# Reordered seam between sample sequences, head norms by logarithm and exponential, token rows by GpSimd's queue and VectorE

## The reference, cut to what matters

```python
def rms_norm(x, g):
    xf = x.astype(F32)
    y = xf * lax.rsqrt(jnp.mean(xf * xf, axis=-1, keepdims=True) + EPS)
    return (y * g.astype(F32)).astype(x.dtype)

k = rms_norm(k.reshape(bsz, L, N_HEADS, 2, HEAD_DK), k_norm)        # head norms of k, q, o
q = rms_norm((h @ w_q).reshape(bsz, L, N_HEADS, 2, HEAD_DK), q_norm)
...
# prompt: causal, 4 blocks of 128 queries; sample: 2048 cached keys and 8 new ones
p = jax.nn.softmax(s, axis=-1)
w = p[:, :, 0] - lam * p[:, :, 1]
o = w @ v
...
o = rms_norm(o, subln) * (1.0 - lam_init)
```

## Time and profile before

| | |
|---|---|
| median of 3 runs | 2074.89 us (2073.44 to 2076.32) |
| the profiled execution, own time | 2083.15 us |
| its span | 2081.3 us |
| PE, PEld, DVE, ACT, POOL busy | 89%, 80%, 40%, 35%, 7% |
| mean granted PE clock | 0.927 |
| `dense("q")`; `qtok` and GpSimd's set-up; attention; `ohead` | 976 to 1024.7; 1024.7 to 1074; 1074 to 1530; 1530 to 1565 us |

### The profile page before, as it was taken

How to read it: one execution, slowest core, us unless ns; L and a number is a source line. 1 busy time by engine, 2 the same in 40 slices (tenths; PEclk the granted TensorE clock), 3 DMA queues, 4 the chain that set the end, 5 groups by cost and what they waited for, 6 DMA issues and landing times.

```text
span 2081.3 us, 42740 instructions
## 1 busy us (share of the span) xinstructions
PE 1851.6 (89%) x17223; PEld 1659.0 (80%) x17223; DVE 839.7 (40%) x1423; ACT 734.0 (35%) x1112; POOL 142.5 (7%) x277
## 2 busy tenths in 40 slices
PE   4798889899999999898868888988758799999998
PEld 2473679799999999798856766666438799999997
DVE  6557223433333233315764444444454433333232
ACT  1433333433333222424346444444131333333212
POOL 2010012200000022101010000000013200000000
PEclk9878899899999999899989999999868799999999
DMA  8758642122222223222158888888651122222222
GB/s 241 261 186 285 210 134 81 51 78 84 81 81 76 70 83 96 61 81 61 61 170 278 324 317 310 306 305 303 217 162 51 51 81 81 81 81 70 82 83 73
DMA packets 245005, 301.03 MB, mean 145 GB/s; under 512 B 10188, under 2 KB 195472, under 8 KB 244816
## 3 DMA queue, kind: packets, MB, share of 16 engines
q1 hardware_dynamic: 241752, 290.22, 42.5%
q10 hardware_dynamic: 2432, 8.16, 1.1%
q0 software_dynamic: 704, 0.95, 0.2%
HBM read 291.92 MB, written 7.37 MB: 144 GB/s over the span
## 4 chain that ended last, share of the span: by engine, by line
PE 71%; DVE 10%; DMA 7%; ACT 4%; SPq 4%; issue 3%; POOL 0%; DVEq 0%; ACTq 0%; POOLq 0%
PE ps L576 55%; PE ps L499 5%; DMA kpg<-in_cache_k 3%; DVE t L1761 2%; SPq L449 2%; DMA raw<-in_w_ada_mix 2%; PE ps L526 2%; SPq L456 2%; PE ps L860 2%; PE ps L715 1%; DMA vpg<-in_cache_v 1%; PE ps L931 1%; DMA raw<-in_w_ada_ffn 1%; ACT kTs L1341 1%; DVE wh L1701 1%
## 5 line engine op out<-in xcount | busy, mean ns | idle before, releaser
L576 PE MATMUL ps<-hr,ws 128*128 128x288 f32 x5760 | 787.2, 299 | 34.8 <-DVE hr L1719 16.9
L576 PEld LDWEIGHTS ps<-hr,ws 128*128 128x128 f32 x5760 | 782.6, 192 | 38.7 <-issue 31.4
L1713 DVE TENSOR_TENSOR ws<-raw,ws 128x1024 fp32r<-128x1024 f32 x200 | 234.8, 1176 | 699.9 <-ACT ws L1189 699.9
L1189 ACT ACTIVATE ws<-raw 128x1024 fp32r<-128x1024 f32 x200 | 201.2, 1008 | 656.9 <-PE ps L576 632.0
L576 PE MATMUL ps<-gr,ws 128*128 128x288 f32 x2112 | 279.4, 294 | 0.0
L576 PEld LDWEIGHTS ps<-gr,ws 128*128 128x128 f32 x2112 | 279.1, 188 | 0.0
L1341 ACT ACTIVATE kTs<-ps 128x512 f32<-128x512 f32 x256 | 141.2, 596 | 165.5 <-PE ps L499 165.1
L499 PE MATMUL ps<-ident,kpg 128*128 128x128 f32 x1024 | 152.7, 298 | 15.7 <-DMA kpg<-in_cache_k 10.6
L499 PEld LDWEIGHTS ps<-ident,kpg 128*128 128x128 f32 x1024 | 123.1, 152 | 46.6 <-issue 23.1
L526 PE MATMUL ps<-raw,cond 128*32 128x256 f32 x896 | 83.5, 482 | 44.7 <-DMA raw<-in_w_ada_mix 34.6
L576 PE MATMUL ps<-hg,ws 128*128 128x288 f32 x768 | 106.2, 302 | 8.9 <-DVE ws L1713 8.9
(11 more groups left out here) (312 smaller groups left out, 1595.2 us busy)
## 6 DMA issues: line engine op xcount, KB each, us to landing
kpg<-in_cache_k SPq DMA_DIRECT2D x128, 512.0 KB, 5.7
vpg<-in_cache_v SPq DMA_DIRECT2D x128, 512.0 KB, 5.9
raw<-in_ffn_w SPq DMA_DIRECT2D x88, 512.0 KB, 3.8
raw<-in_w_ada_mix SPq DMA_DIRECT2D x48, 512.0 KB, 5.4
raw<-in_w_ada_ffn SPq DMA_DIRECT2D x48, 512.0 KB, 4.8
raw<-in_ffn_w SPq DMA_DIRECT2D x48, 384.0 KB, 3.5
raw<-in_w_ada_kv SPq DMA_DIRECT2D x16, 512.0 KB, 5.6
raw<-in_ssm_w_glu SPq DMA_DIRECT2D x16, 512.0 KB, 4.3
```

The lines of the kernel that those rows point to most:

```text
L576: return mm(ps[:, 4 * s + 2 * tile + h, 0:HALF], ws[:, (u * S + j) % 2, w, k, :], src[:, k0 + k, v, h * HALF:(h + 1) * HALF], start=(k0 + ...
L1189: A(ws[:, w, 0, 0:nk, :].rearrange("p k n -> p (k n)"), raw[:, slot, 0:nk, :].rearrange("p k n -> p (k n)"), ACT.Copy).then_inc(slab_high, 1)
L1713: TT(f(ws[:, w, 1, 0:nk, :]), f(raw[:, slot, 0:nk, :]), f(ws[:, w, 0, 0:nk, :]).bitcast(F32), ALU.subtract).then_inc(raw_done[slot], 1)
```

## The change

1. **Head norms.** `head_root` becomes `Ln` (out of PSUM into `t2`), a semaphore wait on `ln_head`, and `Exp` with scale -0.5 in place: exp(-0.5 ln(m + eps)). DVE's `RECIPROCAL` goes, and with it one step.
2. **qtok.** The five V copies go from ACT to DVE, each behind the head norm of the same unit. All ten stores go from ACT's queue to GpSimd's, which issues them in a loop ahead of its set-up for attention. `y` gets its own semaphores.
3. **The seam on PE.** `block_weights` of a head's last block goes to the end of the turn, behind `new_scores(b)`. `outputs(b)` goes behind `turn_page(b+1, 0)` and `turn_weights(b+1, 0)`, which change places. `values(b, 0)` now waits for `o_ready`.
4. **The seam on DVE.** `outputs` is split: `values_out(b)` (L1919) ahead of `bias(b)`, the rest behind `weights(b+1, 0)`. `block_turned` of a head's last block goes to the end of the turn. `normalize` goes from the start of the turn to behind `block_weights` of its first block.

```diff
@@ PE, sequence
+                if keys:
+                    turn_page(b, par, 0)
                 if vals:
                     turn_weights(b, par, 0)
-                if keys:
-                    turn_page(b, par, 0)
+                if b > LAG:
+                    outputs(b - 1)
                 for u in range(PAGES):
...
-                    if u % 4 == 0 and 0 < n <= H * QB:
+                    if u % 4 == 0 and u and 0 < n <= H * QB:
                         block_weights(n - 1)
...
                 if keys:
                     new_scores(b, par)
-                if vals:
-                    outputs(b)
+                if 0 < n0 + QB <= H * QB:
+                    block_weights(n0 + QB - 1)
@@ ACT
             def head_root(n, bank, s, width):
                 act.wait_ge(head_ready, n + 1)
-                return A(halves(t2[:, s, :]), ps[:, bank:bank + 2, 0:HALF], ACT.Sqrt, bias=eps[:, 0:1], scale=1.0 / width)
+                A(halves(t2[:, s, :]), ps[:, bank:bank + 2, 0:HALF], ACT.Ln, bias=eps[:, 0:1], scale=1.0 / width).then_inc(ln_head, 1)
+                act.wait_ge(ln_head, n + 1)
+                return A(t2[:, s, :], t2[:, s, :], ACT.Exp, scale=-0.5)
@@ GpSimd, ahead of its set-up for attention
+            for n in range(2 * (QB + 1)):
+                s, v, i = n % 2, n // (QB + 1), n % (QB + 1)
+                pool.wait_ge(free[s], uses("qtok", s, n // 2) + 1)
...
+                pool.dma_start(rows_.rearrange(form), dst).then_inc(tok_put[i % 2], 16)
@@ DVE
             def head(src, h, s, g):
-                step(REC(t2[:, s, :], t2[:, s, :]))
...
+            for n in range(2 * (QB + 1)):
+                s, v, i = n % 2, n // (QB + 1), n % (QB + 1)
+                if n < H:
+                    dve.wait_ge(root_head, n + 1)
+                    head(qT, n, s, vec[:, 121:122])
+                if v:
+                    wait_unit(dve, "qtok", s, n // 2)
...
+                    if i == QB:
+                        dve.wait_ge(tok_put[i % 2], 16 * 5)
+                    CP(dst, ps[0:NTOK[i], 4 * s + 2:4 * s + 4, :].rearrange("p b c -> p (b c)")).then_inc(free[s], 1)
@@ DVE, sequence
                     weights(b, 0)
-                if 0 < b <= DB:
-                    normalize(b, par)
+                if b > LAG:
+                    outputs(b - 1)
...
-                    if 0 < n <= H * QB:
+                    if q and 0 < n <= H * QB:
                         block_turned(n - 1)
...
                         block_weights(n)
+                    if q == 0 and 0 < b <= DB:
+                        normalize(b, par)
                     if keys:
                         scores(b, par, q)
                 if keys:
                     new_scores(b, par)
+                if vals:
+                    values_out(b)
+                if keys:
                     bias(b)
-                if vals:
-                    outputs(b)
+                if 0 < n + 1 <= H * QB:
+                    block_turned(n)
```

More of the change, by code:

```diff
@@ L924, in values @@
                 if u == 0:
-                    pe.wait_ge(o_copied, b - LAG + 1)
+                    pe.wait_ge(o_ready, b - LAG + 1)
                 if u % 4 == 0:
@@ L981, in sequence @@
                     new_scores(b, par)
-                if vals:
-                    outputs(b)
+                if 0 < n0 + QB <= H * QB:
+                    block_weights(n0 + QB - 1)
             for b in range(DB + LAG):
                 sequence(b)
+            outputs(DB + LAG - 1)
             pe.wait_ge(o_ready, DB + 1)
@@ L1302, in _ @@
                     head_root(H + n, 4 * s, s, DK).then_inc(root_head, 1)
[L1303 to L1309, removed]
+                if not v:
+                    if i >= 2:
+                        act.wait_ge(tok_put[slot], 16 * (i // 2))
+                    A(tok[0:NTOK[i], slot, :], ps[0:NTOK[i], 4 * s + 2:4 * s + 4, :].rearrange("p b c -> p (b c)"), ACT.Copy
+                      ).then_inc(free[s], 1)
                 if n + 2 < H:
                     square(qT, n + 2, s)
[L1312 to L1317, removed]
             def block_exp(n):
@@ L1514, in _ @@
             apply("q")
+            for n in range(2 * (QB + 1)):
+                s, v, i = n % 2, n // (QB + 1), n % (QB + 1)
+                pool.wait_ge(free[s], uses("qtok", s, n // 2) + 1)
+                o_ = out[6 + v] if i < QB else out[8 + v]
+                rows_ = (o_[0, i * P:(i + 1) * P] if i < QB else o_)
+                form = {(0, 0): "t h m d -> t (h m d)", (0, 1): "t h d -> t (h d)", (1, 0): "b t h m d -> (b t) (h m d)",
+                        (1, 1): "b t h d -> (b t) (h d)"}[(int(i == QB), v)]
+                dst = vtok[:, i].rearrange("p h d -> p (h d)") if v and i < QB else tok[0:NTOK[i], i % 2, :]
+                pool.dma_start(rows_.rearrange(form), dst).then_inc(tok_put[i % 2], 16)
             pool.wait_ge(head_ready, 2 + 2 * H)
@@ L1767, in dense @@
                 S, n0 = len(slabs), SLABS[name] - DENSE0
-                steps_ = per * {"glu": 1, "q": 1}.get(name, 0)
+                steps_ = per * {"glu": 1}.get(name, 0)
                 def turn(i, last):
@@ L1829, in _ @@
             dense("q", tail=False)
-            for n in range(H):
-                dve.wait_ge(root_head, n + 1)
-                head(qT, n, n % 2, vec[:, 121:122])
+            for n in range(2 * (QB + 1)):
[5 more added lines that the diff above has]
+                    wait_unit(dve, "qtok", s, n // 2)
+                    dst = vtok[:, i].rearrange("p h d -> p (h d)") if i < QB else tok[0:NTOK[i], i % 2, :]
+                    if i == QB:
+                        dve.wait_ge(tok_put[i % 2], 16 * 5)
+                    CP(dst, ps[0:NTOK[i], 4 * s + 2:4 * s + 4, :].rearrange("p b c -> p (b c)")).then_inc(free[s], 1)
             def block_max(n):
@@ L1914, in weights, with values_out, outputs @@
                 CP(wT[:, q % 2, :], ps[:, 7, :]).then_inc(wt_copied, 1)
-            def outputs(b):
+            def values_out(b):
                 dve.wait_ge(vn_used, b - LAG + 1)
                 CP(osb[:, :], ps[:, 6, 0:2 * DV]).then_inc(o_copied, 1)
+            def outputs(b):
                 dve.wait_ge(o_turned, b - LAG + 1)
@@ L1943, in sequence @@
                     new_scores(b, par)
+                if vals:
+                    values_out(b)
+                if keys:
                     bias(b)
-                if vals:
-                    outputs(b)
+                if 0 < n + 1 <= H * QB:
+                    block_turned(n)
             for b in range(DB + LAG):
                 sequence(b)
+            outputs(DB + LAG - 1)
             split(SLABS["wo"] - DENSE0)
             split(SLABS["wo"] - DENSE0 + 1)
-            with step.loop(0, H // 2, 2) as i:
+            with dve.Fori(0, H // 2) as i:
                 for s in range(2):
```

11 lines of the change are left out of this document (6 added, 5 removed).

## The result

The changed kernel takes 2049.61 us (median of 4 runs, 2047.03 to 2051.1) against 2074.97 before: ratio 0.9877, 95% interval 0.986 to 0.9894. That is 25 us or 1.2% faster; the forecast was 2052. The profiled execution of the changed kernel took 2049.9 us, at its median, while that of before lay 8 us above its own. So I compare stages, not spans. Times of stages are of one profiled execution each.

The account below looks back on a forecast made before the run. PE was taken to bound the attention, with holes at the seams, and DVE's head-norm chains `qtok` and `ohead`. Seams -44.4 and norms with token rows +21.3 gave -23.1, from 2074.9 to 2051.8 us; range 2018 to 2080.

Parts of the forecast that it names:

- Two loads a head: Head norms: `Ln` and `Exp` taken to sit in different tables, so two loads a head, 1.28 us each.
- The slower rival: Table switches hold ScalarE longer than the load's row: 2106 us; chance 0.15, shared with a sum off that far.
- The first pair of the q product, +4.6: In `dense("q")`, loads around the first pair's norms free set 0 at 983.8 in place of 979.2.
- qtok: Norms and token rows: last `Exp` 39.0 us after first `Ln`, first scores +13.5 us, including +4.3 from the first pair.
- ohead: Head norms of the output: ACT at 4.62 or 5.19 us a head, ending 7.8 us later.
- The seams, -48.4: Attention, between turns: the new order removes PE's holes and half clock, gaining 48.4 us over eight seams.
- the walk: PE and DVE followed through seam 4 to 5 at full clock: 7.9 us in place of 15.8; other seams likewise.
- `normalize`, +4.0: Late `normalize` on DVE delays PE's second `block_scores`: 0.4 x 6 = 2.4 us, plus 1.6 in turn 8.
- The rest of the attention: Attention outside the seven seams; the whole attention was forecast at 48.4 - 4.0 = 44.4 us gained.
- The transfers take over: Rival: page loads hold the turn near 51 us, the seams give half, 22: 2074 us; chance 0.13.
- The sum: Whole kernel: -44.4 from the seams and +21.3 from norms and token rows, -23.1 us in all.
- its own range: Likeliest case's range, 2037 to 2073 us: from half clock staying in part and 9.6 of `normalize`, to no stall there.

Follow-up runs that it names:

- e4: The changed kernel with one line more, loading the table with both logarithm and exponential ahead of the q product: 2004.4 us.
- e5: The changed kernel with `normalize` back at the start of the turn, ahead of the first `block_max`: 2044.1 us.
- e0: The kernel before, unchanged, run again for a second profile: 2076.2 us.
- e2: The kernel before with only the head norms changed to logarithm and exponential, token rows left on ScalarE: 2094.3 us.
- e3: The kernel before with only the token rows moved, V copies to DVE and stores to GpSimd's queue: 2083.7 us.
- e1: The kernel before with only the seam's reordering on PE and DVE (parts 3 and 4): 2030.3 us.
- e8: The changed kernel with both the one table loaded ahead and `normalize` at the start of the turn: 2004.4 us.
- e6: The kernel before with only the seam's part for `wtT`, `outputs(b)` staying directly behind `new_scores(b)`: 2046.7 us.
- e9: The changed kernel with one table loaded ahead, `normalize` early, and V copies and their stores back on ScalarE: 1996.4 us.

## Why the prediction was right, step by step

- **Two loads a head.** Right, 48 of them, each 1.283 us with work starting 0.02 behind it. The choice rested on loads being placed without looking ahead; e4 shows that a table with both functions exists and that, with the load placed by hand ahead of the loop, none is placed inside it. The slower rival (a switch costs more than its row) is out: `Ln` starts 1.30 us after its load does (1044.69 to 1045.99), as in rows 10. The Trainium skill (ScalarE: Activation LUTs, section "Table sets: the hidden batching unit") has one load for `ln` then `exp`; the trace of the changed kernel differs, with 48 loads for 24 pairs, and e4, where the set with both is named, agrees with it, with no load in its 24 pairs. The Trainium skill (ScalarE: Activation LUTs, section "What ACT_TABLE_LOAD costs") adds a drain of about 1.38 us to each load; the trace differs, with 1.30 us from the start of a load of 1.28 to the start of `Ln`, and 0.02 from the end of `Ln` to the next load.
- **The first pair of the q product, +4.6.** Measured 4.8, by other parts. The reload at the loop head cost nothing: it ran at 972.0, while ACT waited for PE. The first products resumed 3.2 us later in the stage, and 1.6 more came from the clock: the same 45 products ran at 1.00 before and at a mean of 0.78 behind the longer hole. The changed kernel, then the kernel before:

```profile
972.00 1.28 ACT L1193 ACT_TABLE_LOAD   x1
...
979.50 7.77 PE L577 MATMUL ps<-hr,ws 128*128 128x288 f32 x45 [3.96 <-ACT t L1237]
```

```profile
979.20 6.20 PE L576 MATMUL ps<-hr,ws 128*128 128x288 f32 x45 [0.75 <-DVE ws L1713]
```

- **qtok.** First `Ln` to last `Exp` 39.0 forecast, 39.2 measured (1034.93 to 1074.11); from there to the scores 10.6 and 10.75; in all +13.5 and +13.9.
- **ohead.** +7.8 and +7.8.
- **The seams, -48.4.** Right in mechanism, and near in sum: the seven seams that the walk prices at -47.8 took 99.9 us before and 52.3 after, -47.6. Single seams were off both ways:

| seam (turns) | before, us | after, us | gain forecast | gain measured |
|---|---|---|---|---|
| 1 to 2 | 11.8 | 8.7 | 4.3 | 3.0 |
| 2 to 3 | 13.8 | 6.65 | 6.0 | 7.2 |
| 3 to 4 | 17.0 | 6.65 | 9.1 | 10.3 |
| 4 to 5 | 15.8 | 6.65 | 7.9 | 9.1 |
| 5 to 6 | 15.7 | 6.65 | 7.8 | 9.1 |
| 6 to 7 | 15.7 | 8.2 | 7.8 | 7.5 |
| 7 to 8 | 10.2 | 8.8 | 4.9 | 1.4 |

  Four seams are 1.2 to 1.3 us shorter than forecast, since PE has no gaps between its groups: it is busy 6.60 of 6.60 us, with PEld's 5.34 under it. The forecast had gaps of 1.5 us. (The walk as written does not add up either: from 1299.1 its terms and 1.5 of gaps end at 1306.9, and its 1306.0 leaves 0.6 for them.) The three others are dearer than forecast because the clock was not at full: its mean was 0.80, 0.79 and 0.61, and the last seam's `head_values` took 4.64 us, not 2.4. The first and the last of them also have about 1 us of waits each. The seam from 6 to 7 has no hole at all. Its eight page transposes:

```profile
1376.80 1.91 PE L500 MATMUL ps<-ident,kpg 128*128 128x128 f32 x8
```

  Here are the sums over the seven seams, before and after. The waits in them fell from 32.2 to 2.2 us, and PE's busy time by 17.6:

```profile
sum 99.92, PE 67.69 PEld 50.31 DVE 34.05 ACT 28.13 POOL 2.62; mean PE 9.67 PEld 7.19 DVE 4.86 ACT 4.02 POOL 0.38
```

```profile
sum 52.29, PE 50.12 PEld 39.83 DVE 21.89 ACT 27.25 POOL 2.62; mean PE 7.16 PEld 5.69 DVE 3.13 ACT 3.89 POOL 0.37
```

- **`normalize`, +4.0.** Right in mechanism (DVE's queue, covered in part by page loads). The waits of `block_scores` for `wtT` came to 9.1 us in the attention, after 1.2 before: 0.87 in each of the turns 2 to 7 where I had 0.4, and 3.0 in turn 1, which I had left out. But waits for pages shrank beside them. Outside these seams PE's waits grew by 1.8 us in all (32.6 to 34.4), and undoing the step in e5 saved 1.6 of waits. So the net cost is below the 4.0, not above.
- **The rest of the attention.** Measured -51.2 against -44.4. The missing 6.8 us lie outside the seven seams, where I expected 3.4 us more and the trace has 3.5 less: PE's busy time there fell from 323.7 to 318.5 us for the same products. That need not come from the change. The same stretches kept PE busy for 324.0, 318.1 and 317.7 us in e0, e2 and e3, which have the kernel before's order, and for 320.5 and 320.3 in e1 and e4, which have the changed one. It is the clock, which differs between executions of one order.
- **The transfers take over.** Not in this kernel, but near. The share over a turn is 0.99, and SP issues 29 pages from 1293.83 to 1330.82, one in 1.32 us: for 32 pages 42 of the 45.8 us. (In rows 7 the last load shown is the 29th too, not the thirtieth, so the pace there was 1.31, not 1.26; and the share in rows 8 is 1.02, where the prediction read 1.00.) The waits of e5 and e8 show that most of what the early `normalize` saves inside a turn is lost to the loads.
- **The sum.** Forecast -23.1. By the stages -51.2 + 13.9 + 7.8 = -29.4; by the medians -25.4; e1 and e2 alone, by medians, -45.8 + 18.2 = -27.6. Against e0, whose own time is near the median, the stages give -28.6 and the parts ahead and behind 2.3 back. That the forecast lies within 2.3 us of the median is in part luck: seams off both ways cancelled, and so did, in part, the clock outside the seams and the wandering of parts that no edit touches. The lower end of its own range, 2037, has no sum behind it: no stall at `normalize` leads only to 2048.

## What to carry to other kernels

Cost an activation together with its table: where two functions alternate, count two loads per pair unless a table with both is active, and look at the program for the loads; one load placed by hand was worth 45 us here, more than the whole change. Look at the granted clock when you price a short hole on TensorE: in e6 a hole of 1.8 us cost 4.0 on average, since the clock fell behind it, and in the seams of this change 30.1 us of waits were worth 47.6. Before you look for the cause of a few us, compare PE's busy time and clock for the same products: here they differed by 7 us (e8 and e9) with the waits the same. When an instruction of another engine seems to set the length of a wait, follow what is ahead of it in its own queue: it may move up with the engine that waits.

## What the runs showed of the hardware that I had not expected

- A hole of 1.8 us on TensorE, with small products of 8 columns ahead of it, is followed by half clock for a stretch: in all five seams of e6 from turn 2 to turn 7 (mean clock 0.70 or 0.83). Of the same five seams of the changed kernel, which have no hole, four ran at 1.00. The fifth fell to half clock all the same, behind the same small products (mean 0.79, 8.2 us in place of 6.65). So the hole is not the only cause, and what the other is stays open.
- Page loads ran for six turns at a DMA share of 0.97 and 367 GB/s on average in the changed kernel (in e1, 0.98 and 372 over the same window):

```profile
1144.00:1414.00 270.00, 257.19 (x4310) 203.63 (x4310) 135.20 (x318) 142.50 (x304) 7.87 (x30) 0.99 0.97 367
```

- The part ahead of the q product, with its weight loads from HBM, varied by up to 15 us between profiled executions of code that is the same there.
